# Another order for the first loads of a one-layer encoder step, and the first weight unit split in two halves

## The chip, the cores and the metric

One Trainium2 chip, one of its cores. The metric is device time in microseconds (us) from the first to the last instruction of one launch with what lies around it; lower is better. The engines are named as the profile names them: PE (TensorE, matmuls; PEld is its weight loads), DVE (VectorE), ACT (ScalarE), POOL (GpSimd), SP (SyncE, which here only issues DMAs).

## The reference

320 tokens (256 of a prompt, 64 of a sample with 256 cached positions), width 1024, one layer:

```python
mod = silu(c) @ w_ada + b_ada            # -> sh1, sc1, g1, sh2, sc2, g2, one row per sequence
h = rmsnorm(x, norm1_g) * (1 + sc1) + sh1
proj = h @ w_in                          # A: q|k|v   B: q|k|v   gate_A   gate_B
oa = diff_attention(A's q, k, v)         # 8 heads, two softmax maps each; k, v are outputs too
ob = stick_breaking(B's q, k, v)         # 16 heads
x = x + g1 * ((sigmoid(gate_A) * (oa @ w_oa) + sigmoid(gate_B) * (ob @ w_ob)) @ w_out)
h2 = rmsnorm(x, norm2_g) * (1 + sc2) + sh2
x = x + g2 * hier_moe(h2)                # 4 groups of 8 experts, two experts for each token
```

All is float32. The kernel gets float32 accuracy from fast matmuls by splitting both operands into a rounded high part and the rest (`hi`, `lo`), and adding three products.

## The kernel before

Stages: opening (norm, modulation, first projection), eight heads of A as a software pipeline over heads, gate and output of A, eight pairs of heads of B, output projection, router, experts. The order of the work is written out by hand for each engine; semaphores tie the engines together, and each engine runs its own list strictly in order.

**Opening loads.** SP issues the two conditioning vectors (L351, L352), then eight pieces of `w_ada` of 1 MB each (`load_first`, L360, tile `ada_first`), then unit 1 of `w_in` (`load_unit`, L356, into `raw[1]`). A unit is the q, k and v columns of one head, 1024 rows by 384 columns, loaded by three DMAs of 512 KB whose rows are 512 bytes long. After them SP waits for `setup_done` and issues the router's small loads (L372 to L375), the first cache loads, and, behind the first projection, unit 2. ACT issues the token rows `x_sb` (L1074, L1075), the constants, the bias and the norm vectors (L1076 to L1079); its first computation, the sigmoid of the conditioning (L1082), waits for all six small loads. Behind it ACT issues nine small loads of rows (L1102 to L1105) and then starts the norm of the tokens (`norm_rows`, L1092). POOL issues unit 0 (L1856, into `raw[0]`).

**Opening computation.** PE turns the vectors into columns (L581), multiplies three pieces of `w_ada` (L575 on `ada_first`), transposes the normalised tokens (L586), multiplies the other five pieces as they land, and transposes the result after ACT has copied it (`first_rows`, L1134; L607). DVE makes shift and gain from it (`mod_columns`, L1418, L1421), then the modulated sample tokens (L1465) and the modulated prompt tokens in four blocks, two token tiles `t` by two halves of the 1024 rows (`first_full`, L1454). For each block ACT makes the high part (`hT_hi`, L1141) and DVE the low part (`first_low`, L1462).

**First unit.** Unit 0 is split as a whole ahead of the modulation: ACT makes `w_hi` (`split`, L1119), DVE `w_lo` (L1432). PE then runs `proj_sample` (32 float32 matmuls on `raw`, L575) and `proj_tile` for the two token tiles (24 products of three kinds each, L570 to L572). ACT copies each product to `stage` (L1157 for the sample, L1161 for a tile).

**Second unit.** In ACT's list the steps behind the last `hT_hi` block are: the `hT_hi` block of the sample (L1142), a wait for `lam_sum` and the exponential of it (L1144), the copy of the sample's product, the copy of tile 0's product, then the two halves of unit 1's `w_hi` (L1126, L1130). In DVE's list the steps behind the last `first_low` are the sample's low part (L1477), five small operations on lambda that end in `lam_sum` (L1480 to L1484), and then the two halves of unit 1's `w_lo` (L1440). PE starts unit 1 (`proj_sample(1)`) when both halves of `w_lo` are made.

The lines that the change touches:

Of the kernel before, what the change touches and what calls it, by code (L numbers as in the profile page):

```python
# [7 lines left out]
P = 128  # L8
D = 1024
KD = D // P  # L10
SEQ, DEC, PAST = 256, 64, 256
# [68 lines left out]
def build(nc, t_in, t_out):  # L80
    g = t_in
    ctx = ExitStack()
    with ctx:
        def sem(name):
            return ctx.enter_context(nc.semaphore(name))
# [188 lines left out]

        small_in = sem("small_in"); rows_in = sem("rows_in"); x_in = sem("x_in"); router_in = sem("router_in")
        setup_done = sem("setup_done")
# [62 lines left out]
        def f32(ap):  # L339
            return ap.bitcast(F32)  # L340
# [9 lines left out]
        def _(sp):  # L350
            sp.dma_start(vec_rows[64:72, :], g["c_prompt"].rearrange("a (k p) -> (a k) p", p=P)).then_inc(small_in, 16)  # L351
            sp.dma_start(vec_rows[72:80, :], g["c_sample"].rearrange("a (k p) -> (a k) p", p=P)).then_inc(small_in, 16)  # L352
            def load_unit(base, h, j):
# [14 lines left out]
            for k in range(KD):  # L368
                load_first(k)
            load_unit(0, 1, 1)  # L370
            sp.wait_ge(setup_done, 1)
# [192 lines left out]
        def _(pe):  # L564
# [12 lines left out]
            for s in (e_h, e_h, e_y, e_y, e_hT, e_hT):  # L577
                pe.nop().then_inc(s, 1)

            pe.wait_ge(c_dve, 1)  # L580
            nc.tensor.transpose(ps[:, 0, 0:80], vec_rows[:], ident[0:80, 0:80]).then_inc(col_T, 1)  # L581
# [81 lines left out]
            def proj_tile(h, j, t, first):  # L663
                if first and t == 0:
                    pe.wait_ge(split_done, S_A + 1)
                if not first:
                    pe.wait_ge(a_staged, 3 * h - 1 + t)
                for k in range(KD):
                    sl = slice(t * P, (t + 1) * P)
                    if first and k % 4 == 0:  # L670
                        pe.wait_ge(h_ready, 2 * t + k // 4 + 1)
                    last = mm3(ps[:, t, 0:UNIT], hT_hi[:, k, sl], hT_lo[:, k, sl], w_hi[j][:, k, :], w_lo[j][:, k, :],
                               k == 0, k == KD - 1)
                last.then_inc(a_proj, 1)
# [397 lines left out]
        def _(act):  # L1072
            A = nc.scalar.activation
            act.dma_start(x_sb[:, 0:2, :], g["x_prompt"][0].rearrange("(t p) d -> p t d", p=P)).then_inc(x_in, 16)  # L1074
            act.dma_start(x_sb[0:DEC, 2, :], g["x_sample"][0]).then_inc(x_in, 16)  # L1075
            act.dma_start(cst[:], g["shape_constants"][:, 0:C_ALL]).then_inc(small_in, 16)  # L1076
# [3 lines left out]
            nc.scalar.preload_act_table_set("natural_log_exp_and_others")  # L1080
            act.wait_ge(small_in, 96)
            A(c_sig[64:80, :], vec_rows[64:80, :], ACT.Exp, scale=-1.0).then_inc(c_act, 1)  # L1082
# [13 lines left out]
            def norm_out():  # L1096
                for k in range(0, KD, 2):
                    act.wait_ge(n_T, k + 1)
                    A(xnT[:, k, :], ps[:, k, 0:PADDED], ACT.Copy).then_inc(n_out_a, 1)

            for n, name in enumerate(("a_lam_q1", "a_lam_k1", "a_lam_q2", "a_lam_k2")):
                act.dma_start(lam_rows[:, n, :], g[name].partition_broadcast(P)).then_inc(rows_in, 16)  # L1102
            for n in range(4):
                act.dma_start(gqk[:, n, :], g["a_qnorm_g" if n < 2 else "a_knorm_g"].partition_broadcast(P)).then_inc(rows_in, 16)
            act.dma_start(subln[:], g["a_subln_g"].rearrange("(p a) -> p a", a=1)).then_inc(rows_in, 16)  # L1105
            act.wait_ge(setup_done, 1)
            act.wait_ge(x_in, 32)
            norm_rows(xn)
            norm_out()

            def split(j, loaded, used, width=UNIT):

                if loaded is None:
                    act.wait_ge(unit0_in, 48)
                else:
                    act.wait_ge(raw_loaded[j], loaded - 48 * (1 - j))
                if used is not None:
                    act.wait_ge(*used)
                A(w_hi[j][:, :, 0:width], raw[j][:, :, 0:width], ACT.Copy).then_inc(split_hi, 1)  # L1119
# [11 lines left out]

            split(0, None, None)
            act.wait_ge(ada_used, KD)
            A(first_rows[:], ps[:, 7, :], ACT.Copy).then_inc(n_out_a, 1)  # L1134

            act.wait_ge(mod_ready, 1)
            for t in range(2):
                for half in range(2):
                    ks = slice(4 * half, 4 * half + 4)
                    act.wait_ge(h_mod, 2 * t + half + 2)  # L1140
                    A(hT_hi[:, ks, t * P:(t + 1) * P], h_full[:, ks, t * P:(t + 1) * P], ACT.Copy).then_inc(h_hi, 1)  # L1141
# [235 lines left out]
        def _(dve):  # L1377
# [65 lines left out]

            split(0, 0)
            dve.wait_ge(col_T, 2)
# [20 lines left out]
            last.then_inc(h_mod, 1)  # L1466
            first_full(0, 0)
            first_full(0, 1)
            for t in range(2):
                first_low(t, 0)  # L1470
                if t == 0:
                    first_full(1, 0)
                first_low(t, 1)
                if t == 0:
                    first_full(1, 1)
            dve.wait_ge(h_hi, 5)
# [338 lines left out]
        def _(pool):  # L1815
# [38 lines left out]

            for n in range(3):
                pool.dma_start(raw[0][:, :, n * P:(n + 1) * P], w_in3[:, :, n * D:n * D + P]).then_inc(unit0_in, 16)  # L1856

            pool.wait_ge(n_T, KD)
# [134 lines left out]
```

## Time and profile before

| what | us |
|---|---|
| median of three runs | 822.73 |
| these runs | 819.91, 822.73, 823.5 |
| the profiled execution | 823.22 |
| its span, first to last instruction | 821.4 |

The span is 1.8 us shorter than the time of the same execution. The profile lists for each instruction its start and its duration, the tile that it writes and those that it reads, the idle time ahead of it on its engine, and what ended that. Of DMAs it gives the issue on the issuing engine's queue (SPq, ACTq), the bytes moved per stretch, and the time to landing of some. The granted clock is that of PE: 1.00 is 2.4 GHz, and 0.5 is 1.2 GHz; a value between them is a mean over a stretch that holds both.

### The profile page before, as it was taken

To read this page: it belongs to the slowest core of one execution; us is meant where nothing else is said; L and a number is where in the kernel's file an instruction comes from. 1 tells how busy PE (TensorE), PEld (TensorE's weight loads), DVE (VectorE), ACT (ScalarE), POOL (GpSimd) and SP (SyncE) were. 2 spreads that over 40 slices of the span, in tenths; PEclk is the share of its full clock that TensorE was granted. 3 is DMA by queue.
4 is the path that set the end of the run, shared out by engine and by line. 5 is a ranking of instruction groups with operands and counts; after the bars stand their busy time and mean duration, and the time that the engine had idled before them with its cause. 6 is when DMAs were issued, how large, how long until landed. Compare 5 with 4: busy or idle time off the path is not lost.

```text
span 821.4 us, 13826 instructions
## 1 busy us (share of the span) xinstructions
PE 702.3 (85%) x5345; PEld 565.7 (69%) x5345; DVE 352.0 (43%) x552; ACT 270.8 (33%) x500; POOL 94.7 (12%) x158
## 2 busy tenths in 40 slices
PE   0798899998799999999988999878999897788770
PEld 0387788887689999999978999755565444454430
DVE  1555767777443433444323356542423232223225
ACT  0444555554443445554334542300111011011110
POOL 2012222222000000001100000011011001100011
PEclk9899999999999999999988999878999999999995
DMA  9957377764636795332315447789799999999916
GB/s 320 340 149 227 121 233 216 223 213 134 206 103 181 186 290 150 106 105 80 94 33 165 128 132 286 278 356 358 303 417 417 417 417 419 417 418 417 385 67 192
DMA packets 131176, 199.17 MB, mean 242 GB/s; under 512 B 11688, under 2 KB 113464, under 8 KB 117816
## 3 DMA queue, kind: packets, MB, share of 16 engines
q1 hardware_dynamic: 123032, 185.63, 63.9%
q0 software_dynamic: 6208, 11.02, 4.0%
q10 hardware_dynamic: 1888, 1.86, 0.8%
q8 instruction: 32, 0.52, 0.3%
q14 instruction: 16, 0.13, 0.0%
HBM read 193.47 MB, written 16.55 MB: 256 GB/s over the span
## 4 chain that ended last, share of the span: by engine, by line
PE 41%; DMA 16%; DVE 13%; ACT 10%; issue 8%; SPq 4%; DVEq 4%; ACTq 2%; POOL 1%; POOLq 0%
PE ps L575 18%; DMA e_w<-in_w 14%; PE ps L570 7%; PE ps L572 6%; PE ps L571 6%; ACT w_hi L1119 4%; SPq L507 3%; DVE w_lo L1432 2%; DMA vec_rows<-in_norm_g 2%; DVE w_lo L1440 1%; ACT probs L1217 1%; SPq L512 1%; DVE amap L1501 1%; ACT sig_r L1236 1%; ACT probs L1188 1%
## 5 line engine op out<-in xcount | busy, mean ns | idle before, releaser
L575 PE MATMUL ps<-e_w,xgT 128*64 128x256 f32 x1024 | 127.5, 408 | 27.8 <-issue 19.8
L575 PEld LDWEIGHTS ps<-e_w,xgT 128*64 128x64 f32 x1024 | 83.3, 147 | 67.7 <-issue 24.8
L570 PE MATMUL ps<-hT_hi,w_hi 128*128 128x320 f32 x320 | 102.4, 320 | 4.4 <-DVE w_lo L1432 4.2
L1432 DVE TENSOR_TENSOR w_lo<-raw,w_hi 128x2048 fp32r<-128x2048 f32 (+1 forms) x26 | 68.1, 2619 | 81.1 <-ACT w_hi L1119 81.1
L572 PE MATMUL ps<-hT_hi,w_lo 128*128 128x320 f32 x320 | 99.5, 311 | 0.0
L571 PE MATMUL ps<-hT_lo,w_hi 128*128 128x320 f32 x320 | 99.4, 311 | 0.0
L1764 DVE TENSOR_SCALAR h_s<-h_e 128x256 f32<-128x256 f32 x16 | 4.7, 294 | 156.0 <-ACT h_e L1349 156.0
L570 PEld LDWEIGHTS ps<-hT_hi,w_hi 128*128 128x128 f32 x320 | 60.7, 190 | 7.1 <-issue 4.0
L1119 ACT ACTIVATE w_hi<-raw 128x2048 fp32r<-128x2048 f32 (+1 forms) x26 | 56.4, 2168 | 21.7 <-PE ps L572 21.7
L571 PEld LDWEIGHTS ps<-hT_lo,w_hi 128*128 128x128 f32 x320 | 60.8, 190 | 0.0
L572 PEld LDWEIGHTS ps<-hT_hi,w_lo 128*128 128x128 f32 x320 | 60.7, 190 | 0.0
L575 PE MATMUL ps<-e_w,hidT 128*64 128x512 f32 x256 | 58.4, 598 | 0.6 <-ACT hidT L1355 0.6
L1349 ACT ACTIVATE h_e<-ps 128x256 f32<-128x256 f32 x16 | 6.1, 384 | 146.5 <-PE ps L575 146.5
L570 PE MATMUL ps<-w_hi,hT_hi 128*128 128x384 f32 x128 | 44.1, 344 | 0.0
L572 PE MATMUL ps<-w_hi,hT_lo 128*128 128x384 f32 x128 | 42.9, 335 | 0.0
L571 PE MATMUL ps<-w_lo,hT_hi 128*128 128x384 f32 x128 | 42.8, 335 | 0.0
L570 PE MATMUL ps<-oT_hi,w_hi 128*128 128x320 f32 x128 | 39.9, 312 | 1.1 <-DVE oT_lo L1602 1.1
L1939 POOL DMA_INDIRECT expert_rows<-y_sb,idx x16 | 16.1, 1008 | 208.3 <-DVE y_sb L1777 194.1
L572 PE MATMUL ps<-oT_hi,w_lo 128*128 128x320 f32 x128 | 39.6, 309 | 0.0
L571 PE MATMUL ps<-oT_lo,w_hi 128*128 128x320 f32 x128 | 39.6, 309 | 0.0
L575 PEld LDWEIGHTS ps<-e_w,hidT 128*64 128x64 f32 x256 | 17.2, 136 | 29.9 <-issue 28.0
L1440 DVE TENSOR_TENSOR w_lo<-raw,w_hi 128x1536 fp32r<-128x1536 f32 (+1 forms) x20 | 33.1, 1698 | 7.6 <-ACT w_hi L1126 7.6
(260 smaller groups left out, 1267.6 us busy)
## 6 DMA issues: line engine op xcount, KB each, us to landing
e_w<-in_w SPq DMA_DIRECT2D x96, 1024.0 KB, 23.3
raw<-in_w_in SPq DMA_DIRECT2D x45, 512.0 KB
ada_late<-in_w_ada SPq DMA_DIRECT2D x16, 1024.0 KB, 6.4
ada_first<-in_w_ada SPq DMA_DIRECT2D x8, 1024.0 KB, 21.5
raw<-in_w_in SPq DMA_DIRECT2D x8, 1024.0 KB
raw<-in_w_oa SPq DMA_DIRECT2D x4, 1024.0 KB
raw<-in_w_ob SPq DMA_DIRECT2D x4, 1024.0 KB
raw<-in_w_out SPq DMA_DIRECT2D x4, 1024.0 KB
```

The source lines that it names most:

```text
L507: sp.dma_start(ew[2 * q + half][w][:], g[name].rearrange("e (p k) f -> e p k f", k=KD)[2 * p + half]).then_inc(landed[q], 16)
L512: sp.dma_start(ew[2 * q + half][2][:], g["w2"].rearrange("e (p m) d -> e p m d", m=2)[2 * p + half]).then_inc(w2_in[q], 16)
L570: nc.tensor.matmul(out, lhs_hi, rhs_hi, start=first, stop=False, skip_group_check=True)
L571: nc.tensor.matmul(out, lhs_hi, rhs_lo, start=False, stop=False, skip_group_check=True)
L572: return nc.tensor.matmul(out, lhs_lo, rhs_hi, start=False, stop=last, skip_group_check=True)
L575: return nc.tensor.matmul(out, lhs, rhs, start=first, stop=last, skip_group_check=True)
L1119: A(w_hi[j][:, :, 0:width], raw[j][:, :, 0:width], ACT.Copy).then_inc(split_hi, 1)
L1188: last = A(probs[mp][:, 384:704], ps[:, 5 + mp, 0:320], ACT.Exp, bias=a_nmx[:, mp, 2:3], accum_out=a_sum[:, mp, 2:3])
L1217: last = A(probs[mp][:, sl], ps[:, 5 + mp, sl], ACT.Exp, bias=a_nmx[:, mp, t:t + 1], accum_out=a_sum[:, mp, t:t + 1])
L1432: V.tensor_tensor(w_lo[j][:, :, 0:width], raw[j][:, :, 0:width], f32(w_hi[j][:, :, 0:width]), ALU.subtract).then_inc(split_done, 1)
L1440: last = V.tensor_tensor(w_lo[j][:, ks, 0:width], raw[j][:, ks, 0:width], f32(w_hi[j][:, ks, 0:width]), ALU.subtract)
L1939: G.indirect_dma_start(y_dram, bass.IndirectOffsetOnAxis(ap=idx[:, 1, p:p + 1], axis=0), y_sb[j][:], None, bounds_check=2 * TOK, oob_is_er ...
```

## The change

The token rows are issued first on SP, ahead of `w_ada`, and the conditioning vectors first on ACT. Unit 0 goes from POOL to SP, behind the eight pieces of `w_ada` and ahead of unit 1. ACT's sigmoid waits for the conditioning alone, and PE waits for the other four small loads ahead of its first transposes. ACT's nine small loads are issued behind `norm_rows`. The split of unit 0 moves behind the modulation, in two halves of its rows: ACT makes a half of `w_hi` ahead of each of the first two `hT_hi` blocks, DVE a half of `w_lo` ahead of each of the first two `first_low` blocks. The blocks of token tile 1 now follow one by one, `first_full` and `first_low` of a half, then of the next.

```diff
         @block.sync
-            sp.dma_start(vec_rows[64:72, :], g["c_prompt"].rearrange("a (k p) -> (a k) p", p=P)).then_inc(small_in, 16)
-            sp.dma_start(vec_rows[72:80, :], g["c_sample"].rearrange("a (k p) -> (a k) p", p=P)).then_inc(small_in, 16)
+            sp.dma_start(x_sb[:, 0:2, :], g["x_prompt"][0].rearrange("(t p) d -> p t d", p=P)).then_inc(x_in, 16)
+            sp.dma_start(x_sb[0:DEC, 2, :], g["x_sample"][0]).then_inc(x_in, 16)
...
             for k in range(KD):
                 load_first(k)
+            for n in range(3):
+                sp.dma_start(raw[0][:, :, n * P:(n + 1) * P], w_in3[:, :, n * D:n * D + P]).then_inc(unit0_in, 16)
             load_unit(0, 1, 1)
         @block.tensor
+            pe.wait_ge(small_in, 64)
             pe.wait_ge(c_dve, 1)
...
                 if first and t == 0:
-                    pe.wait_ge(split_done, S_A + 1)
+                    pe.wait_ge(unit0_half, 2)
...
                     if first and k % 4 == 0:
+                        if t == 0 and k == 4:
+                            pe.wait_ge(split_done, S_A + 1)
         @block.scalar
-            act.dma_start(x_sb[:, 0:2, :], g["x_prompt"][0].rearrange("(t p) d -> p t d", p=P)).then_inc(x_in, 16)
-            act.dma_start(x_sb[0:DEC, 2, :], g["x_sample"][0]).then_inc(x_in, 16)
+            act.dma_start(vec_rows[64:72, :], g["c_prompt"].rearrange("a (k p) -> (a k) p", p=P)).then_inc(c_in, 16)
+            act.dma_start(vec_rows[72:80, :], g["c_sample"].rearrange("a (k p) -> (a k) p", p=P)).then_inc(c_in, 16)
...
-            act.wait_ge(small_in, 96)
+            act.wait_ge(c_in, 32)
...
+            act.wait_ge(setup_done, 1)
+            act.wait_ge(x_in, 32)
+            norm_rows(xn)
             for n, name in enumerate(("a_lam_q1", "a_lam_k1", "a_lam_q2", "a_lam_k2")):
...
-            act.wait_ge(setup_done, 1)
-            act.wait_ge(x_in, 32)
-            norm_rows(xn)
             norm_out()
...
-            split(0, None, None)
             act.wait_ge(ada_used, KD)
             A(first_rows[:], ps[:, 7, :], ACT.Copy).then_inc(n_out_a, 1)
-            act.wait_ge(mod_ready, 1)
+            act.wait_ge(unit0_in, 48)
             for t in range(2):
                 for half in range(2):
                     ks = slice(4 * half, 4 * half + 4)
+                    if t == 0:
+                        A(w_hi[0][:, ks, :], raw[0][:, ks, :], ACT.Copy).then_inc((unit0_half, split_hi)[half], 1)
                     act.wait_ge(h_mod, 2 * t + half + 2)
                     A(hT_hi[:, ks, t * P:(t + 1) * P], h_full[:, ks, t * P:(t + 1) * P], ACT.Copy).then_inc(h_hi, 1)
         @block.vector
-            split(0, 0)
             dve.wait_ge(col_T, 2)
...
             first_full(0, 0)
+            dve.wait_ge(unit0_half, 1)
+            V.tensor_tensor(w_lo[0][:, 0:4, :], raw[0][:, 0:4, :], f32(w_hi[0][:, 0:4, :]), ALU.subtract).then_inc(unit0_half, 1)
+            first_low(0, 0)
             first_full(0, 1)
-            for t in range(2):
-                first_low(t, 0)
-                if t == 0:
-                    first_full(1, 0)
-                first_low(t, 1)
-                if t == 0:
-                    first_full(1, 1)
+            dve.wait_ge(split_hi, 1)
+            V.tensor_tensor(w_lo[0][:, 4:8, :], raw[0][:, 4:8, :], f32(w_hi[0][:, 4:8, :]), ALU.subtract).then_inc(split_done, 1)
+            first_low(0, 1)
+            for half in range(2):
+                first_full(1, half)
+                first_low(1, half)
         @block.gpsimd
-            for n in range(3):
-                pool.dma_start(raw[0][:, :, n * P:(n + 1) * P], w_in3[:, :, n * D:n * D + P]).then_inc(unit0_in, 16)
```

## Rows read from the trace of the kernel before

**Rows 1.** The chain that ended last, 30 to 56 us: start us, us, what.

```profile
31.11 2.66 ACT w_hi L1119
33.79 3.36 DVE w_lo L1432
37.69 1.89 DVE xnT L1465 x8
...
48.63 0.49 ACT stage L1161
49.13 1.39 ACT w_hi L1126
50.60 3.44 DVE w_lo L1440 x2
```

**Rows 2.** Stretches of the opening; the last three columns: PE's clock, DMA share, GB/s.

```profile
0.00:2.00 2.00, 0.00 (x0) 0.00 (x0) 0.00 (x0) 0.00 (x0) 1.26 (x10) 1.00 0.12 14
...
6.00:22.00 16.00, 2.33 (x13) 0.86 (x17) 2.13 (x6) 1.70 (x4) 0.56 (x1) 1.00 1.01 359
22.00:32.50 10.50, 8.02 (x56) 4.93 (x52) 4.31 (x7) 5.70 (x11) 0.77 (x2) 0.84 1.04 412
33.00:38.70 5.70, 3.12 (x28) 0.83 (x20) 4.65 (x8) 1.36 (x2) 0.00 (x0) 1.00 1.14 286
```

**Rows 3.** DMA issues of the first 20 us: tile, queue, count, KB each, us to landing.

```profile
ada_first<-in_w_ada SPq DMA_DIRECT2D x8, 1024.0 KB, 21.5
raw<-in_w_in POOLq DMA_DIRECT2D x3, 512.0 KB, 13.8
```

**Rows 4.** Timeline: PE and weight loads, start us, us; in brackets idle before and releaser.

```profile
34.39 0.16 PEld L575 LDWEIGHTS ps<-ada_first,c_cols 128*32 128x32 f32 x8 [0.82 <-DMA ada_first<-in_w_ada]
39.71 4.50 PE L575 MATMUL ps<-raw,xnT 128*64 128x192 f32 x32 [2.87 <-DVE xnT L1465]
54.09 2.82 PE L575 MATMUL ps<-raw,xnT 128*64 128x192 f32 x32 [1.33 <-DVE w_lo L1440]
70.45 4.50 PE L575 MATMUL ps<-raw,xnT 128*64 128x192 f32 x32 [2.31 <-DVE w_lo L1440]
```

**Rows 5.** Timeline of DVE, 37 to 54 us, columns as in rows 4.

```profile
37.07 0.19 DVE L1418 TENSOR_TENSOR mod<-ps,vec_cols 128x32 f32<-128x32 f32 x1
...
39.47 2.14 DVE L1454 TENSOR_SCALAR h_full<-xnT,gain,mod 128x128 f32<-128x128 f32 x8
41.52 0.69 DVE L1462 TENSOR_TENSOR hT_lo<-h_full,hT_hi 128x512 fp32r<-128x512 f32 x1
42.12 1.11 DVE L1454 TENSOR_SCALAR h_full<-xnT,gain,mod 128x128 f32<-128x128 f32 x4
...
46.18 0.68 DVE L1477 TENSOR_TENSOR hT_lo<-xnT,hT_hi 128x512 fp32r<-128x512 f32 x1
...
47.40 0.28 DVE L1484 TENSOR_REDUCE lam_sum<-lam_prod 128x2 f32<-128x128 f32 x1
```

**Rows 6.** Timeline of ACT, columns as in rows 4.

```profile
20.61 1.06 ACT L1092 ACTIVATE xn<-x_sb 128x1024 f32<-128x1024 f32 x1 [4.02 <-issue]
...
41.65 0.63 ACT L1141 ACTIVATE hT_hi<-h_full 128x512 fp32r<-128x512 f32 x1 [0.33 <-DVE h_full L1454]
...
47.72 0.20 ACT L1144 ACTIVATE lam_exp<-lam_sum 128x2 f32<-128x2 f32 x1 [1.67 <-DVE lam_sum L1484]
47.83 0.65 ACT L1157 ACTIVATE stage<-ps 64x192 f32<-64x192 f32 x2
```

**Rows 7.** SP's DMA issues, merged: start us, us.

```profile
5.79 28.80 SPq L356 DMA_DIRECT2D raw<-in_w_in  x3
34.64 2.98 SPq L372 DMA_DIRECT2D rw<-in_w_rg  x1
```

**Rows 8.** Granted clock in stretches of PE's sample products, columns as in rows 2.

```profile
39.71:44.20 4.49, 4.49 (x33) 4.05 (x33) 4.49 (x16) 1.89 (x3) 0.00 (x0) 0.62 0.47 108
54.09:56.90 2.81, 2.81 (x33) 2.27 (x33) 0.95 (x1) 0.07 (x1) 0.00 (x0) 1.00 0.03 6
```

## What was predicted

> **What bounds the kernel now.** I read the chain that ended last first, cut to the opening, since the change touches nothing behind unit 1. From 31 us on it runs through the split of unit 0 on ACT and DVE, the modulated sample tokens, PE's products of unit 0, ACT's copy of tile 0's product, the split of unit 1, and unit 1's start on PE at 54.09 us [rows 1, 4]. Behind that I take everything as shifted by what unit 1's start is shifted: PE is busy from there to the first transposes, and the split of unit 2 and its products follow those.
>
> The split of unit 0 stands on the chain only by a hair. PE had waited 0.82 us for the last piece of `w_ada`, which was there at 34.39 us [rows 4]; copy and transposes end about when the split on DVE ends (33.79 + 3.36 = 37.15 us), and the modulation starts at 37.07 us [rows 1, 5]. So two things end together: loads and split.
>
> Then the DMA view by stretches. The engines are busy (share 1.01 to 1.14) all the way to 38.7 us [rows 2]. The opening is a question of which bytes come first: eight pieces of 1 MB of `w_ada`, 1.5 MB of unit 0 on POOL's queue beside them, the tokens, the small loads [rows 3]. While unit 0 was in flight (6 to 22 us) 359 GB/s were moved, behind it 412 GB/s, and at 33 to 38.7 us, when SP's unit 1 came, 286 GB/s [rows 2]. Units are dear for their size.
>
> Last the timelines of DVE and ACT from 37 us. DVE is busy from the modulation at 37.07 us to `lam_sum`, which ends at 47.68 us (47.40 + 0.28) [rows 5]; ACT's exponential of it starts at 47.72 us, the copy of the sample's product at 47.83 us, that of tile 0 at 48.63 us, unit 1's split at 49.13 us [rows 1, 6]. PE, DVE and ACT thus arrive at unit 1's split together. A reader should see that DVE has no room there.
>
> **The change part by part.**
>
> *Small loads and norm earlier.* The sigmoid and norm (20.61 us) [rows 6] come some 10 us earlier. PE still waits for `w_ada`, so this is worth nothing on the path. Its price is nothing too: the nine small loads of ACT stand behind the norm, some 4.0 us of issue (the idle ahead of the norm before [rows 6]), and ACT has nothing due before the token transposes. If that cover were gone, at most those 4.0 us would delay copies that are due ahead of the last `w_ada` piece, which lands over 10 us later. The new wait of PE on the four small loads has only the first transpose behind it and is as well covered. On SP two issues (tokens) take the place of two (conditioning) ahead of `w_ada`; the tokens' 1.3 MB went ahead of most of `w_ada` before too, on ACT's queue, so `w_ada` isn't put back.
>
> *Unit 0 leaves the stretch ahead of `w_ada`'s end.* What it cost there isn't shown alone. Lower bound: its 1.57 MB at the clean rate, 1.57 / 0.412 = 3.8 us. Upper: all of the slower stretch is its doing, 3.8 + 16 x (1 - 359/412) = 5.9 us. I take 1.57 / 0.286 = 5.5 us, from the row with the same shape of load on SP [rows 2], nearer the upper end. The last `w_ada` piece is then there at 34.39 - 5.5 = 28.9 us, and the modulation starts 37.07 - 34.39 = 2.68 us later, M = 31.6 us (before 37.07). That is the gain: 5.5 us.
>
> *Unit 0 comes behind `w_ada`.* On SP's queue it costs the same 5.5 us, so it is there at U = 28.9 + 5.5 = 34.4 us: the same bytes, the last of them now unit 0's. With the two bounds above U lies between 34.0 and 36.1 us. Unit 1 follows 5.5 us later, 39.9 us, and is needed far behind that. SP's list is held in the queue as now (three issues took 28.80 us [rows 7]); its last unit load can go out when five of six are nearly through, and the router's loads follow as they did at 34.64 us before. Unit 2 stands behind them and behind the sample's product, and is due only when unit 1 is through. So SP gives nothing back and costs nothing.
>
> By the Trainium skill, page "DMA: Bandwidth & Descriptors", section "Where 436 GB/s comes from", an HBM load binds at about 358 GB/s for a core. The trace moved 412 GB/s over 10.5 us [rows 2], so I don't take it; by it, as an estimate, the last `w_ada` piece would be 2.6 us later than in my sum, and the end 826.9 us.
>
> *The split on the path.* For unit 1, DVE begins its split 1.47 us behind ACT's start on the first half (49.13 to 50.60 us [rows 1]); so here it can begin 1.5 us behind U. DVE is ready for it when `first_full` of block (0,0) is issued: M + 2.40 (37.07 to 39.47) + 1.03 (half of the eight, 39.47 to 41.52) = M + 3.43 = 35.0 us [rows 5]. U + 1.50 = 35.9 us is later, so A = 35.9 us is where DVE's split of half 0 starts, set by unit 0's arrival and no more by the modulation.
>
> *From A to unit 1, on DVE and ACT.* DVE's steps in its new order: half of the split 1.67, low block 0.60, `first_full` (0,1) 1.03, half of the split 1.67, low block 0.60, `first_full` (1,0) 1.03 (A + 6.60). Now a round trip that was hidden before: ACT makes the high block only when DVE has ended, 0.63 us and two hand-overs, 0.81 [rows 6]; low block 0.60, `first_full` (1,1) 1.03, the second round trip 0.80, low block 0.60 (A + 10.44), sample and lambda 1.50 (46.18 to 47.68): `lam_sum` ends at A + 11.94. Half a split is half of 3.44 us [rows 1], blocks are from start to start in rows 5. ACT: exponential at A + 11.98, sample copy A + 12.09, tile 0's copy A + 12.66, DVE's split of unit 1 1.97 us after that (48.63 to 50.60), unit 1 on PE 3.49 us later (50.60 to 54.09) [rows 1, 4], at A + 18.12 = 54.0 us. Before: 54.09 us, which is M + 17.02. So 5.5 us won ahead of M, and of these 0.8 us are lost waiting for unit 0 and 4.5 us (18.12 + 3.43 - 17.02) because the split and two round trips now stand between M and `lam_sum`. Left: -0.1 us. PE itself hides: tile 0 ends near A + 8.2 and tile 1 near A + 13, both ahead of ACT's need.
>
> *PE waits longer ahead of unit 1.* It is idle from about A + 13 to A + 18.1, 5 us; before it was 1.33 us. The same 32 sample matmuls took 2.82 us behind 1.33 us of idle, at a granted clock of 1.00 (2.4 GHz), but 4.50 us behind idle of 2.31 and of 2.87 us, where the stretch has 0.62, so mostly 1.2 GHz [rows 4, 8]. The new idle is nearest to the two long ones: +1.68 us, on the path, with bounds 0 and 1.68.
>
> **Sum.** 54.0 - 54.09 + 1.68 = +1.6 us. Against the profiled execution (span 821.4 us, time 823.22 us) that makes 824.8 us. Its time lies 0.5 us above the median of the three runs, 822.73 us; against the median it is 824.3 us.
>
> **The rivals.**
>
> *(a) The same, but PE's clock isn't lost.* The clock stood at 1.00 after 1.33 us of idle; if 5 us leave it there too, 822.6 us. Against it: rows 4 and 8.
>
> *(b) The gain is kept.* DVE's work and the round trips are hidden as before, and unit 1 starts at M + 17.02 = 48.6 us: 822.7 - 5.5 = 817.2 us, or 818.9 us with the clock lost. For it: this is what would follow if DVE had idle time between M and `lam_sum`. Against it: it had none [rows 5], and ACT's list puts tile 0's copy and unit 1's split behind the exponential.
>
> *(c) Slower: unit 0 arrives late.* Mechanism: SP can't issue all of the six unit loads while `w_ada` fills its queue; the third issue hung until 34.6 us, 0.2 us behind the landing of the last `w_ada` piece [rows 4, 7]. If now the two later loads of unit 0 each come behind an empty queue, which costs up to 2 us (in the first 2 us of the span all but nothing flows, 14 GB/s [rows 2]), U = 34.4 + 4 = 38.4 us, and A, hence the end, moves by as much: 828.3 us with the clock lost. It decides from U = 33.5 us on, since beyond that every microsecond of U is one of A; slower by over 0.5% from U = 36.9 us on. Against it: in 33 to 38.7 us the queue stayed busy, at a share of 1.14 [rows 2], with a load issued that late.
>
> *(d) The slower rate stays.* The 359 GB/s of 6 to 22 us aren't unit 0's doing but hold for all ahead of `w_ada`'s end: 10.2 MB (8.4 of `w_ada`, 1.3 of tokens, 0.5 small) take 28.4 us, from 2 us on to 30.4 us, landed about 1.1 us behind the flow (before: rate falling near 33 us, landed at 34.39 us), 31.5 us instead of 28.9: the end is 2.6 us later, 826.9 us. Against it: 412 GB/s from 22 us on with `w_ada` alone [rows 2].
>
> **How the numbers follow.** My forecast (gain eaten, clock lost) 0.53; (a) 0.20; (b) 0.10; (c) 0.14; (d) 0.03. Predicted: 824.3 us. What a measurement of this kernel can tell from no change is about 0.5%, 4.1 us: 818.6 to 826.8 us. Forecast and (a) lie within; with the bounds of U (-0.4, +1.7) the forecast goes from 823.9 to 826.0 us, (a) from 822.2 to 824.3 us. The single runs spread from 819.91 to 823.5 us. Faster by over 0.5%: most of (b), 0.08. Slower by over 0.5%: (c), half of (d) and a little of the forecast's upper end, 0.18. Same: 0.74. The range leaves out (b) and the farther part of (c): 820.5 to 828.0 us.
>
> **What would show it.** In the profile after: last `w_ada` piece at about 29 us and the modulation near 31.6 us (else the bytes were mis-costed); unit 0 on PE at about 34.4 us (later: (c)); DVE waiting for ACT ahead of the split's first half and ahead of the low blocks of tile 1; `lam_sum` near 47.8 us; unit 1's sample product near 54 us, with 4.5 us of duration (2.8 us: (a)). If unit 1 starts ahead of 51 us, the step from A to unit 1 is wrong, and (b) holds.

## The result and the profile after

| | median us | range of the runs | runs |
|---|---|---|---|
| before | 821.13 | 817.96 to 824.26 | 20 |
| changed | 825.77 | 821.62 to 828.69 | 20 |

The ratio is 1.0056, 95% interval 1.0039 to 1.0072: the change costs 4.6 us. The time lies in the forecast range and on the side to which the forecast leaned (+1.6 us), but the loss is three times as large as that. The time itself lies only 1.5 us above the forecast 824.3 us, and that is partly luck: the forecast stood on the median of the first three runs before, 822.73 us, which is 1.6 us above that of all twenty. The profiled execution of the changed kernel has a span of 825.9 us and took 827.69 us, 4.5 us more than that of before.

The chain that ended last, in the opening of the changed kernel (start us, us, what); it answers to [rows 1]:

```profile
24.33 11.75 DMA raw<-in_w_in
36.10 1.49 ACT w_hi L1142
37.62 1.76 DVE w_lo L1471
...
44.34 0.64 ACT hT_hi L1144
45.00 0.69 DVE hT_lo L1464
...
46.76 0.64 ACT hT_hi L1144
47.42 0.69 DVE hT_lo L1464
...
49.26 0.30 DVE lam_sum L1488
49.59 0.20 ACT lam_exp L1147
...
50.76 1.48 ACT w_hi L1128
52.33 3.44 DVE w_lo L1443 x2
55.81 4.20 PE ps L577 x27
```

The modulation is no longer on it. The chain comes from the third DMA of unit 0, goes through the split, through two round trips between ACT and DVE for the blocks of tile 1, through lambda, and only then to unit 1. Before, it went from the modulated sample over PE's products to ACT's copy of tile 0.

PE and its weight loads in the changed kernel's timeline (start us, us; idle before and releaser in brackets), which answer to [rows 4]:

```profile
29.50 0.16 PEld L577 LDWEIGHTS ps<-ada_first,c_cols 128*32 128x32 f32 x8 [2.65 <-DMA ada_first<-in_w_ada]
36.13 4.13 PE L577 MATMUL ps<-raw,xnT 128*64 128x192 f32 x32 [4.18 <-DMA raw<-in_w_in]
55.81 4.52 PE L577 MATMUL ps<-raw,xnT 128*64 128x192 f32 x32 [5.28 <-DVE w_lo L1443]
73.85 5.39 PE L577 MATMUL ps<-raw,xnT 128*64 128x192 f32 x32 [2.32 <-DVE w_lo L1443]
93.79 2.82 PE L577 MATMUL ps<-raw,xnT 128*64 128x192 f32 x32 [1.54 <-DVE w_lo L1443]
```

Unit 3 in the kernel before:

```profile
89.20 2.82 PE L575 MATMUL ps<-raw,xnT 128*64 128x192 f32 x32 [1.54 <-DVE w_lo L1440]
```

The last `w_ada` piece is there 4.9 us earlier (29.50 us, before 34.39). Unit 0 is there at 36.1 us, and unit 1 starts 1.7 us later than before (55.81 us, before 54.09). Its sample product takes 1.7 us longer. Unit 2 starts 3.4 us late (before 70.45 us), its product is longer too, and unit 3 starts at 93.79 us, 4.6 us later than before, when it started at 89.20 us. That is the whole difference of the two profiled times (4.5 us): between these two profiles nothing is won or lost behind it. That they agree so well there is partly luck. The time of the profiled execution less the start of unit 3 is 734.0 and 733.9 us for these two, but over all the profiles of this document it goes from 730.3 to 735.1 us, though no edit lies behind unit 3's start. A difference of two single profiles is therefore not to be taken to the microsecond; the medians decide, and they differ by 4.6 us.

The granted clock in the three last of these products (last three columns: clock, DMA share, GB/s), which answer to [rows 8]:

```profile
55.81:60.30 4.49, 4.49 (x33) 3.26 (x33) 0.81 (x1) 0.00 (x0) 0.00 (x0) 0.61 0.02 4
73.85:79.20 5.35, 5.35 (x34) 3.66 (x34) 3.25 (x11) 2.45 (x9) 0.00 (x0) 0.50 0.47 167
93.79:96.60 2.81, 2.81 (x33) 2.27 (x33) 1.75 (x5) 0.83 (x5) 0.00 (x0) 1.00 0.00 0
```

### The profile page after: what moved, and what is told of

Its sections match the earlier page's. It is cut to its first block, busy times and chain, and to the rows that moved or that the text cites. A ratio compares the mean times of both kernels' runs of the same rounds, so it can differ in the third digit from the quotient of the medians.

```text
span 825.9 us, 13829 instructions
## 1 busy us (share of the span) xinstructions
PE 698.9 (85%) x5345; PEld 560.2 (68%) x5345; DVE 352.3 (43%) x553; ACT 270.9 (33%) x501; POOL 92.3 (11%) x155
## 4 chain that ended last, share of the span: by engine, by line
PE 40%; DMA 17%; DVE 12%; ACT 9%; issue 8%; SPq 7%; DVEq 4%; ACTq 2%; POOL 1%; POOLq 0%
PE ps L577 18%; DMA e_w<-in_w 14%; PE ps L572 6%; PE ps L574 6%; PE ps L573 6%; ACT w_hi L1121 4%; SPq L509 3%; SPq L371 2%; DVE w_lo L1435 2%; DMA raw<-in_w_in 1%; DVE w_lo L1443 1%; ACT probs L1220 1%; DMA yb<-expert_rows 1%; SPq L514 1%; DVE amap L1505 1%
## 5 line engine op out<-in xcount | busy, mean ns | idle before, releaser
L577 PE MATMUL ps<-e_w,xgT 128*64 128x256 f32 x1024 | 124.1, 400 | 31.2 <-issue 19.6
L577 PEld LDWEIGHTS ps<-e_w,xgT 128*64 128x64 f32 x1024 | 80.8, 144 | 70.2 <-issue 26.1
L1435 DVE TENSOR_TENSOR w_lo<-raw,w_hi 128x2048 fp32r<-128x2048 f32 (+1 forms) x25 | 64.7, 2589 | 77.4 <-ACT w_hi L1121 77.4
L1121 ACT ACTIVATE w_hi<-raw 128x2048 fp32r<-128x2048 f32 (+1 forms) x25 | 53.6, 2145 | 21.7 <-PE ps L574 21.7
L577 PE MATMUL ps<-raw,xnT 128*64 128x192 f32 x256 | 28.2, 384 | 13.3 <-DVE w_lo L1443 9.1
```

The lines of the kernel that those rows point to most:

```text
L577: return nc.tensor.matmul(out, lhs, rhs, start=first, stop=last, skip_group_check=True)
L1435: V.tensor_tensor(w_lo[j][:, :, 0:width], raw[j][:, :, 0:width], f32(w_hi[j][:, :, 0:width]), ALU.subtract).then_inc(split_done, 1)
```

## The experiments

Each experiment is a kernel of its own, timed against the kernel before on the same chip; the ratios are to those runs, whose median was 820.97 to 822.17 us from series to series. The first four test the terms of the sum, the next ones look for the cause of what was off.

**Tokens and small vectors alone.** The kernel before, with only these parts of the change: tokens first on SP, conditioning first on ACT, sigmoid and norm earlier, the nine small loads behind the norm. Unit 0 and its split are as before. The diff is against the kernel before.

```diff
-            act.wait_ge(small_in, 96)
+            act.wait_ge(c_in, 32)
...
+            norm_rows(xn)
             for n, name in enumerate(("a_lam_q1", "a_lam_k1", "a_lam_q2", "a_lam_k2")):
```

> Only the tokens on SP, the small vectors on ACT, the earlier sigmoid and norm; unit 0 stays on POOL and its split ahead of the modulation. Theory (the opening ends with the last piece of w_ada and nothing ahead of that is on the path): the same time as before, 821 us within 1 us; modulation at 36.9 to 37.1 us. Rival (the earlier norm is a gain of its own): the modulation comes over 1 us earlier, 820 us or less.

Measured: 821.08 us, ratio 0.9998 (0.9978 to 1.0018); the modulation starts at 37.04 us, as before. This part is worth nothing, within 0.2%.

**Unit 0 alone.** The changed kernel with tokens and small vectors as before; of the diff against the kernel before:

```diff
+            for n in range(3):
+                sp.dma_start(raw[0][:, :, n * P:(n + 1) * P], w_in3[:, :, n * D:n * D + P]).then_inc(unit0_in, 16)
             load_unit(0, 1, 1)
```

> Only unit 0 behind w_ada on SP and the split in halves behind the modulation; tokens and small vectors as before. Theory (this part alone makes the loss): like the changed kernel, 825 to 827 us, unit 0 landed near 36 us, unit 1 on PE near 55.8 us with 4.5 us for its sample product. Rival (the moved tokens and small loads are part of the loss): 823 us or less.

Measured: 825.45 us, ratio 1.0044 (1.0025 to 1.0064); unit 0 is there at 36.5 us, unit 1 starts at 56.22 us and its product takes 4.71 us. The whole loss, within the intervals, is in this part.

**PE filled ahead of unit 1.** The changed kernel with seven matmuls whose result nothing reads, behind unit 0's products.

```diff
+            def filler(count):
+                for n in range(count):
+                    nc.tensor.matmul(ps[:, 6, 0:384], ident, cst[:, 0:384], start=True, stop=True, skip_group_check=True)
...
+                if isinstance(h, int) and h == 0:
+                    filler(7)
```

> The changed kernel, with seven extra float32 matmuls of 384 columns on PE behind unit 0's products, into a bank that nothing reads then; they fill most of the 5.3 us in which PE waits for unit 1's split. Theory (the long sample product is PE's clock, lost in that idle time): unit 1's sample product takes 2.8 us instead of 4.5, and unit 2's 4.5 instead of 5.4; 822.9 to 824.1 us. Rival (the product is long for another reason, its operands or the DMAs): 4.5 us and 825.8 us as without them.

Measured: 822.81 us, ratio 1.0023 (1.0003 to 1.0043). PE's timeline (the seven matmuls are recorded as 14 instructions):

```profile
50.99 4.68 PE L683 MATMUL ps<-cst 128*128 128x384 f32 x14
56.43 2.82 PE L577 MATMUL ps<-raw,xnT 128*64 128x192 f32 x32 [0.76 <-DVE w_lo L1449]
72.78 4.21 PE L577 MATMUL ps<-raw,xnT 128*64 128x192 f32 x32 [2.32 <-DVE w_lo L1449]
```

The stretches of the two products (last three columns: clock, DMA share, GB/s):

```profile
56.43:59.20 2.77, 2.77 (x33) 2.22 (x33) 0.81 (x1) 0.00 (x0) 0.00 (x0) 1.00 0.02 6
72.78:76.95 4.17, 4.17 (x34) 3.07 (x34) 2.16 (x8) 2.45 (x9) 0.00 (x0) 0.66 0.67 239
```

Work that computes nothing makes the changed kernel faster by some 2.7 us (1.0056 to 1.0023). The same product, of the same operands, takes 2.82 us at a clock of 1.00 (2.4 GHz) when PE was busy ahead of it, and 4.52 us when PE had been idle for 5.28 us. So the price of the longer wait is the clock's, as predicted.

**Unit 0 early, split late.** The changed kernel with unit 0 loaded by POOL again, while the split stays behind the modulation.

```diff
-            for n in range(3):
-                sp.dma_start(raw[0][:, :, n * P:(n + 1) * P], w_in3[:, :, n * D:n * D + P]).then_inc(unit0_in, 16)
...
+            for n in range(3):
+                pool.dma_start(raw[0][:, :, n * P:(n + 1) * P], w_in3[:, :, n * D:n * D + P]).then_inc(unit0_in, 16)
             pool.wait_ge(n_T, KD)
```

> The changed kernel with unit 0 loaded by POOL again, as before: it lands early, while the split stays behind the modulation in halves. Theory (the order on DVE and ACT costs 4.5 us behind the modulation, whatever the loads do): last w_ada piece near 34.4 us, modulation near 36.9 us, the first half of the split starts on DVE 3.4 us behind that, unit 1 on PE 21.5 us behind the modulation, 58.4 us; with the clock lost 827 to 829 us. Rival (the loss of the changed kernel is unit 0's late landing alone): unit 1 at 54 us, 821 to 823 us.

Measured: 827.19 us, ratio 1.0072 (1.0053 to 1.0091). Modulation, split and unit 1:

```profile
37.86 0.19 DVE L1419 TENSOR_TENSOR mod<-ps,vec_cols 128x32 f32<-128x32 f32 x1 [8.46 <-PE ps L608]
41.29 1.75 DVE L1469 TENSOR_TENSOR w_lo<-raw,w_hi 128x1536 fp32r<-128x1536 f32 x1
...
59.47 4.98 PE L575 MATMUL ps<-raw,xnT 128*64 128x192 f32 x32 [5.26 <-DVE w_lo L1441]
```

The modulation starts at 37.86 us, 1 us later than expected, the split 3.43 us behind it (41.29 us), unit 1 21.61 us behind it (59.47 us). The order on DVE and ACT costs what the prediction had worked out (21.55 us where it was 17.02), with no late load in play. The run also sizes unit 0's place: with unit 0 on POOL the last `w_ada` piece is used from 34.93 us, with unit 0 behind it from 29.51 us, so unit 0 ahead of `w_ada`'s end costs 5.4 us, where the prediction took 5.5.

**All full blocks first.** The changed kernel with DVE's four `first_full` blocks ahead of the split, in the time in which it waits for unit 0.

```diff
-            first_full(0, 0)
+            for t in range(2):
+                for half in range(2):
+                    first_full(t, half)
             dve.wait_ge(unit0_half, 1)
...
-            first_full(0, 1)
...
             for half in range(2):
-                first_full(1, half)
                 first_low(1, half)
```

> The changed kernel with all four first_full blocks ahead of the split on DVE, in the time in which DVE waits for unit 0. Theory (two hidden round trips and idle time on DVE are what the order costs): the split starts near 38.5 us, 0.9 us later than in the changed kernel, but lam_sum ends near 45.7 us instead of 49.6, and unit 1 starts on PE near 52 us instead of 55.8; PE is idle for about 2.5 us ahead of it and its product takes 4.5 us: 820.5 to 822.5 us. Rival (the path to unit 1 runs over unit 0's landing and PE's tiles, not over lam_sum): unit 1 no earlier than 55 us, 825 us or more.

Measured: 820.25 us, ratio 0.9984 (0.9965 to 1.0003). DVE's split and `lam_sum`, and unit 1 on PE:

```profile
38.48 1.75 DVE L1473 TENSOR_TENSOR w_lo<-raw,w_hi 128x1536 fp32r<-128x1536 f32 x1
...
45.46 0.28 DVE L1488 TENSOR_REDUCE lam_sum<-lam_prod 128x2 f32<-128x128 f32 x1
...
52.01 2.82 PE L577 MATMUL ps<-raw,xnT 128*64 128x192 f32 x32 [2.25 <-DVE w_lo L1443]
```

The split starts 0.9 us later than in the changed kernel, and unit 1 3.8 us earlier, as expected to 0.1 us. The loss is gone with nothing but another order on DVE; the median is 0.25 us below the expected range. Only the clock came out otherwise: the product took 2.82 us, at a clock of 1.00, behind 2.25 us of idle. So some 1.7 us of what was won are the clock's, and they came with the shorter wait.

**Lambda ahead of the modulation.** The kernel with all full blocks first, with the lambda operations of DVE and ACT moved to where DVE waits for `w_ada`.

```diff
+            dve.wait_ge(rows_in, 144)
...
             dve.wait_ge(col_T, 2)
...
+            act.wait_ge(lam_dve, 1)
+            A(lam_exp[:], lam_sum[:], ACT.Exp).then_inc(lam_act, 1)
             act.wait_ge(ada_used, KD)
             A(first_rows[:], ps[:, 7, :], ACT.Copy).then_inc(n_out_a, 1)
```

> The kernel of e5_blocks_first with the lambda operations of DVE and ACT moved ahead of the modulation, where DVE waits for w_ada. Theory: ACT's copy of tile 0 then waits for PE alone, at about 45.3 us; unit 1 starts near 50.7 us, behind some 1.3 us of idle on PE, and its product takes 2.8 us: 816.5 to 819 us. Rival (the lambda chain was beside the path): as e5_blocks_first within 0.7 us.

Measured: 820.74 us, ratio 0.9974 (0.9955 to 0.9993): no better. ACT's two steps and the modulation:

```profile
32.30 0.20 ACT L1135 ACTIVATE lam_exp<-lam_sum 128x2 f32<-128x2 f32 x1 [8.87 <-DVE lam_sum L1453]
32.41 0.58 ACT L1137 ACTIVATE first_rows<-ps 128x512 f32<-128x512 f32 x1
...
33.94 0.19 DVE L1421 TENSOR_TENSOR mod<-ps,vec_cols 128x32 f32<-128x32 f32 x1 [1.01 <-PE ps L610]
```

Lambda came onto the path in another place: the small loads, issued by 15 us, were there only after 31 us, and held up `first_rows` (30.64 us in the changed kernel) and with it the modulation by 2 us. My step had not asked when these loads land.

**Two full blocks first.** The kernel with lambda ahead of the modulation, with only tile 0's two blocks ahead of the split. The lines as they stand in this kernel:

```diff
             first_full(0, 0)
             first_full(0, 1)
...
             for half in range(2):
                 first_full(1, half)
             for half in range(2):
                 first_low(1, half)
```

> The kernel of e6_lambda_early with only the two blocks of token tile 0 ahead of the split and those of tile 1 behind it. Theory: the split starts at 37.6 us, when ACT's first half is there, tile 0 ends on PE 0.9 us earlier than in e6_lambda_early, and so does unit 1's start: near 49.8 us; 815.5 to 818 us. Rival (PE's tile 1 or DVE is late next): no better than e6_lambda_early.

Measured: 819.37 us, ratio 0.9978 (0.9958 to 0.9998). The modulation is later still than in the kernel that it starts from (34.63 us, there 33.94), and unit 1 starts at 52.99 us (there 53.06); the median misses the expected 815.5 to 818 us. Counted from the modulation, unit 1 starts 18.4 us behind it, in the kernel that it starts from 19.1 us: this order is 0.8 us shorter, 0.9 had been expected, and the late modulation takes it back.

**Unit 1 held back.** The changed kernel, with SP waiting for unit 0 to land before it issues unit 1. Unit 0 had landed 1.7 us later than predicted, and I blamed unit 1 beside it.

```diff
+            sp.wait_ge(unit0_in, 48)
             load_unit(0, 1, 1)
```

> The changed kernel, with SP issuing unit 1 only when unit 0 has landed. Theory (unit 0 landed at 36.1 us instead of 34.4 because DMA engines that were through with their part of it took up unit 1 and so held up the others): unit 0 lands at 34.3 to 35 us, unit 1's start and the end come 1 to 1.7 us earlier, 824 to 825 us. Rival (one slow DMA engine or the late issue of the third load sets it, unit 1 is no cause): 36 us as before, 825.8 us.

Measured: 824.77 us, ratio 1.0050 (1.0030 to 1.0071); unit 0 is there at 36.07 us. The theory falls, although the median lies in the range that went with it: unit 0 lands as in the changed kernel, and unit 1 starts at 55.78 us, as there. But with unit 1 away the stretches show how unit 0 ends (the last three columns: clock, DMA share, GB/s), and, in the second fence, the rows of its DMA queues for 27 to 36 us (packets, MB, share of 16 engines; q1 is SP's, q10 is ACT's) show what else was under way:

```profile
33.00:34.00 1.00, 0.00 (x0) 0.00 (x0) 1.00 (x5) 0.00 (x0) 0.00 (x0) 0.70 1.13 285
34.00:35.00 1.00, 0.00 (x0) 0.00 (x0) 1.00 (x5) 0.00 (x0) 0.00 (x0) 0.50 0.27 71
35.00:36.00 1.00, 0.00 (x0) 0.00 (x0) 0.34 (x2) 0.00 (x0) 0.00 (x0) 0.50 0.14 35
```

```profile
q1 hardware_dynamic: 3200, 2.10, 81.7%
q10 hardware_dynamic: 664, 0.12, 7.4%
q8 instruction: 1, 0.02, 0.8%
```

The bulk is through at 34 us; for two more microseconds a few engines work on alone. SP's queue takes 27.3% of the 16 engines from 34 to 35 us, some four of them, and 6.5% from 35 to 36 us, about one; the rest of the 0.14 there is the one packet of q8, which is none of unit 0's. ACT's queue moves 664 packets of small loads for 0.12 MB, and all of them ahead of 31 us: from 28 to 30 us they take 29.6% of the engines, in the last five microseconds nothing. So they are not under way beside the end; if they make it late, it is by what they took before.

**Small loads away.** The changed kernel with ACT's nine small loads issued behind the last `hT_hi` block. It is a single run, for the landings alone: its end, 834.01 us, is late because lambda waits for these loads (unit 1 starts at 61.70 us).

```diff
-            for n, name in enumerate(("a_lam_q1", "a_lam_k1", "a_lam_q2", "a_lam_k2")):
-                act.dma_start(lam_rows[:, n, :], g[name].partition_broadcast(P)).then_inc(rows_in, 16)
...
             A(hT_hi[:, :, SEQ:TOK], h_sample, ACT.Copy).then_inc(h_hi, 1)
+            for n, name in enumerate(("a_lam_q1", "a_lam_k1", "a_lam_q2", "a_lam_k2")):
+                act.dma_start(lam_rows[:, n, :], g[name].partition_broadcast(P)).then_inc(rows_in, 16)
...
```

> The changed kernel with ACT's nine small loads issued behind the last hT_hi block, about 47 us, so that they are away from the stretch in which w_ada and unit 0 are loaded; this look is for the landings alone, and the end comes later, since lambda then waits for these loads. Theory (the last DMA engines finish unit 0 some 1.6 us behind the others because they also carry the small loads): unit 0 lands at 34 to 35 us. Rival (the small loads are no cause, some engines are slower by themselves): unit 0 lands at 35.5 to 36.3 us, the last piece of w_ada at 28.5 to 29.1 us.

Measured: the last `w_ada` piece is used from 28.06 us, the modulation starts at 30.53 us, unit 0 is there at 33.5 us. Unit 0 came even earlier than expected. PE's timeline; then, in the second fence, the landing of unit 0 and of `gqk` (four of the small loads) in the changed kernel, and in the third the same two in this one, in us from the issue:

```profile
28.06 1.06 PE L577 MATMUL ps<-ada_first,c_cols 128*32 128x512 f32 x8 [1.40 <-DMA ada_first<-in_w_ada]
33.50 4.12 PE L577 MATMUL ps<-raw,xnT 128*64 128x192 f32 x32 [3.00 <-DMA raw<-in_w_in]
```

```profile
DMA to landing us min/median/max: 11.7/26.3/27.6
DMA to landing us min/median/max: 15.9/16.1/16.2
```

```profile
DMA to landing us min/median/max: 10.5/23.6/25.0
DMA to landing us min/median/max: 4.1/4.4/5.5
```

The nine loads, eight of 32 KB in rows of 256 bytes and one of 0.5 KB, cost `w_ada` 1.4 us and unit 0 2.6 us, for a quarter of a megabyte. The three kernels that have them out of the way agree: unit 0 is there at 33.4 to 33.5 us in this one and the two in which SP issues them (below), and at 36.1 to 36.7 us in all eight others in which it is loaded behind `w_ada`. The small loads themselves take 16 us to land beside the large loads and 4.4 us here, at the end of a unit's load and behind it.

**Lambda behind unit 1's split.** The kernel with all full blocks first, and lambda moved behind the first head's iteration on DVE and ACT.

```diff
                 a_iteration(h, h % 2, h >= 1, h >= 2, h >= 3, True)
+                if h == 0:
+                    dve.wait_ge(rows_in, 144)
...
```

> The kernel of e5_blocks_first with the lambda operations of DVE and ACT moved behind unit 1's split, so that they wait for nothing on the path and delay nothing there. Theory (what is late ahead of unit 1 is the order on DVE and ACT, and e6_lambda_early lost its gain only because the small loads landed after 31 us and held up first_rows): modulation at 32 us as in the changed kernel, split from 38.5 us, tile 0 copied by ACT when PE has it, at about 45.3 us, unit 1 on PE near 50.7 us with 2.8 us of product: 3 to 5 us under the kernel before, 816 to 818.5 us. Rival (PE's clock and unit 2 take it back): no better than e5_blocks_first, 820 us or more.

Measured: 818.06 us, ratio 0.9960 (0.9940 to 0.9980). ACT's copy of tile 0 now waits for PE:

```profile
46.41 0.49 ACT L1162 ACTIVATE stage<-ps 128x384 f32<-128x384 f32 x1 [3.69 <-PE ps L574]
...
51.87 2.82 PE L577 MATMUL ps<-raw,xnT 128*64 128x192 f32 x32 [1.33 <-DVE w_lo L1444]
```

It comes 1.1 us later than expected, half of it from a modulation at 32.48 us, the rest mostly from PE's sample product of unit 0, which took 5.39 us and so put off tile 0. Otherwise the steps hold.

**Small loads on SP, behind unit 1.** The changed kernel, with the nine loads issued by SP where they follow the large ones.

```diff
             load_unit(0, 1, 1)
+            for n, name in enumerate(("a_lam_q1", "a_lam_k1", "a_lam_q2", "a_lam_k2")):
+                sp.dma_start(lam_rows[:, n, :], g[name].partition_broadcast(P)).then_inc(rows_in, 16)
...
-            for n, name in enumerate(("a_lam_q1", "a_lam_k1", "a_lam_q2", "a_lam_k2")):
-                act.dma_start(lam_rows[:, n, :], g[name].partition_broadcast(P)).then_inc(rows_in, 16)
...
```

> The changed kernel with the nine small loads issued by SP behind unit 1, so that they move only when unit 0 has landed. Theory (the small loads beside w_ada and unit 0 made unit 0 land 2.6 us later than its bytes need): modulation at 30.5 us, unit 0 at 33.5 us, unit 1 on PE near 53.2 us, the end 2.6 us earlier than in the changed kernel, 822 to 824 us. Rival (unit 0's landing isn't on the path): 825.8 us as before.

Measured: 821.37 us, ratio 0.9995 (0.9979 to 1.0011). Unit 0 and unit 1 on PE:

```profile
33.53 4.55 PE L582 MATMUL ps<-raw,xnT 128*64 128x192 f32 x32 [2.83 <-DMA raw<-in_w_in]
...
53.22 4.94 PE L582 MATMUL ps<-raw,xnT 128*64 128x192 f32 x32 [5.27 <-DVE w_lo L1443]
```

The modulation starts at 30.74 us, unit 0 is there at 33.5 us, unit 1 starts at 53.22 us, all as expected; the median is 0.6 us below the range that was expected. This alone takes the loss back, within the interval, with the order on DVE and ACT left as it is. The median is 4.4 us under that of the changed kernel, more than the 2.6 us by which unit 1 starts earlier; in this profile the products of units 1 and 2 are together 0.7 us shorter (4.94 and 4.25 us), and where the rest was won the runs don't say. No run moves the small loads in the kernel before, so how much they cost there is not shown.

**Both.** Full blocks first, lambda behind unit 1's split, small loads on SP.

> The kernel of e9_lambda_behind_unit1 with the nine small loads issued by SP behind unit 1. Theory (both losses, the order on DVE and ACT and the late landings, are apart and add up): modulation at 30.5 us, split from 37.0 us, unit 1 on PE near 49.9 us, 815 to 817 us, 4 to 6.5 us under the kernel before. Rival (in this order the modulation alone sets the path and something else holds it, or lambda's loads come late): no better than e9_lambda_behind_unit1, 818 us or more.

Measured: 816.91 us, ratio 0.9938 (0.9915 to 0.9960): 5.1 us under the kernel before by the ratio, and the lowest of all. Modulation, split and unit 1:

```profile
30.44 0.19 DVE L1422 TENSOR_TENSOR mod<-ps,vec_cols 128x32 f32<-128x32 f32 x1 [5.99 <-PE ps L615]
...
36.95 1.75 DVE L1474 TENSOR_TENSOR w_lo<-raw,w_hi 128x1536 fp32r<-128x1536 f32 x1
...
49.55 2.82 PE L582 MATMUL ps<-raw,xnT 128*64 128x192 f32 x32 [1.33 <-DVE w_lo L1444]
```

At unit 1's start the two losses are apart and add up: the order wins 3.9 us there (51.87 us, changed kernel 55.81), the small loads 2.6 us (53.22 us), both together 6.3 us. In the times they add up only in part: each alone is 5 to 8 us under the changed kernel by the ratios, both together are 9.7 us under it, and against lambda behind unit 1's split alone the intervals overlap (0.9915 to 0.9960 and 0.9940 to 0.9980).

## Why the prediction came out as it did

| step | predicted | measured |
|---|---|---|
| last `w_ada` piece there | 28.9 us | 29.5 us |
| modulation starts, M | 31.6 us | 31.98 us |
| unit 0 there, U | 34.4 us (34.0 to 36.1) | 36.1 us |
| unit 0 behind the last `w_ada` piece | 5.5 us | 6.6 us (5.4 without the small loads) |
| DVE's split starts, A | U + 1.5 us | U + 1.5 us (37.62) |
| unit 1 starts on PE | A + 18.12 us | A + 18.19 us (55.81) |
| unit 1's sample product | 4.50 us | 4.52 us |
| unit 2's sample product | as before, 4.50 us | 5.39 us |
| sum | +1.6 us | +4.6 us |

*Right, and shown by an edit.* The tokens and small vectors moved earlier bring nothing (ratio 0.9998). The order on DVE and ACT eats the gain: the way from A to unit 1 was worked out to 0.1 us, the experiment with unit 0 loaded early gave the same way behind another start, and taking the round trips out of it (all full blocks first) moved unit 1 by 3.8 us. The clock is lost in the wait: with PE filled the product was short again. That the way from A came out to 0.1 us owes a little to luck: half of a split is 1.72 us by the row that the prediction names and not 1.67 (1.68 and 1.67 were measured), and tile 0's copy starts 0.67 us behind the sample's, where the prediction has 0.57 and shows no row for it.

*The term that was mis-sized: unit 0's landing.* The step held that unit 0 lands when the same bytes are through, 34.4 us. It came at 36.1 us, at the very end of its bounds, and since A hangs on it, all of the 1.7 us came out at unit 1. Of these, 0.6 us are the last `w_ada` piece (29.5 us where 28.9 was predicted) and 1.1 us unit 0 behind it (6.6 us where 5.5 was). Nearly all of unit 0 was through at 34 us (seen with unit 1 held back), but its last packets came up to two microseconds later, and ACT's nine small loads, which the sum had as hidden with a price of nothing, were the cause: without them U is 33.5 us. I had asked what ACT's issue of them holds up, and not what they do to the loads that they share the engines with. The last `w_ada` piece felt them too: without them it is used from 28.06 us. That they are why it came 4.9 us earlier and not 5.5 is not shown, since in the kernel before they were loaded beside `w_ada` as well (so the 412 GB/s that the prediction took as `w_ada` alone weren't quite that). The modulation, M, came 5.1 us earlier: it follows the last piece by 2.5 us, not by 2.7 as before, where the split on DVE ended only then. How the small loads put off the end of unit 0 is shown in part. From 18 to 28 us the two queues sent as many packets as each other, 538 for 4.00 MB on SP's and 536 for 0.12 MB on ACT's, so the small loads moved at the pace of the large ones; from 11 to 31 us ACT's queue took 6.7% of the 16 engines' time, which is 1.3 us of all of them. That the rest of the 2.6 us is the uneven end is likely but not shown. The traces don't name the engines that ended last, nor why those; that stays open.

*A term that was left out, but may be small: unit 2's product.* I took everything behind unit 1 as shifted whole. Unit 2 does start behind the same idle time as before (2.32 and 2.31 us), but its product took 5.39 us, and from unit 2's start to unit 3's it is 19.94 us where it was 18.75 us: 1.2 us that no step had. With PE filled ahead of unit 1 it was 4.21 us, in the kernel with lambda early 2.82 us, with all blocks first 5.39 us again, behind the same 2.32 us of idle each time. So this is no fixed price of the change but one that differs from profile to profile. In the two other kernels with the same order and unit 0 equally late the products of units 1 and 2 took 4.71 and 4.14 us (unit 0 alone) and 5.23 and 4.40 us (unit 1 held back): against the 2.82 and 4.50 us before, 1.5 and 2.3 us lost to the clock in all, in the changed kernel 2.6 us, where the forecast had 1.68. How much of the 1.2 us is in the median the runs don't settle.

*The sum.* 1.72 (unit 1's start) + 1.70 (its product) + 1.2 (unit 2 to unit 3) = 4.6 us, from the two profiles; it is also the difference of the medians, but with what single profiles differ by, that it fits to 0.1 us is chance. The forecast's 1.58 us lacked 1.8 us of the first and, in these profiles, 1.2 us of the last. By the prediction's own mark of 0.5% the ratio of 1.0056 lies just beyond no change, on the side to which it gave 0.18.

*The rivals.* That the clock isn't lost (a) is refuted by the product's length and by the filled PE. That the gain is kept (b) fails on the way from A, as stated. A late unit 0 (c) did happen, 1.7 us of it, but not by its mechanism: there was no gap between unit 0's loads (262 to 298 GB/s in every microsecond from 28 to 36 us), and holding unit 1 back changed nothing. The slower rate (d) fails: from 18 to 28 us the changed kernel moved 412 GB/s. The limit of about 358 GB/s that the Trainium skill states (page "DMA: Bandwidth & Descriptors", section "Where 436 GB/s comes from") is not seen here either.

## What to carry to other kernels

When the last load of a stage is put off, ask for its landing and not for its bytes, and count the small loads of other queues that share the engines with it: a quarter of a megabyte, nearly all of it in rows of 256 bytes, cost 2.6 us here. A step that is moved behind a wait takes its place in two lists, its own engine's and that of whoever answers it; where the wait leaves an engine idle, put the work there that waits for nothing, and put what nobody needs yet (lambda here) behind the next engine's start. A wait can cost more than itself: here the product behind PE's longer wait took 1.7 us more, at a granted clock of 0.61 instead of 1.00.

## What the runs showed of the hardware that was not expected

- Small loads on one queue slow large loads on another far beyond their bytes: 0.26 MB cost unit 0 2.6 us, while at 412 GB/s they would take 0.6 us. Beside `w_ada` the two queues' packets went out one for one (538 and 536 from 18 to 28 us) whatever their size, and the small loads landed after 16 us; away from it after 4.4 us.
- A load's end is uneven over the engines: with nothing behind it, unit 0 went at 285 GB/s from 33 to 34 us; then its queue held 27.3% of the 16 engines for one microsecond (71 GB/s) and 6.5% for the next.
- Behind nearly the same idle time PE's clock had fallen in some profiles and not in others. The sample product took 2.82 us, at a granted clock of 1.00, behind 2.25 us of idle (all full blocks first), 2.32 us (lambda ahead of the modulation) and 2.68 us (unit 0's, with tokens and small vectors alone), but 4.58 us behind 2.68 us (unit 0's, with lambda ahead of the modulation). Behind 2.31 or 2.32 us it took 4.1 to 5.4 us in the other profiles, at 0.66 with PE filled (4.21 us) and 0.50 in the changed kernel (5.39 us). In the kernel before it was 2.82 us behind 1.33 and 1.54 us, with two full blocks first 2.82 us behind 1.90 us. The idle time given is only the last one ahead of the product. A single profile of this kernel can therefore stand up to 2.6 us off for one such product alone.
